# Expert routing rebuilt: logits from the raw residual, norm applied token by token, residual finished inside the first expert

## The reference, cut to what matters

```
mix = (sigmoid(..) * y_attn + sigmoid(..) * y_conv) @ w_out[1]
h = layer_norm(ALPHA * h + mix, ln1_g[1], ln1_b[1])      # called n11 in the kernel
logits = h @ router                                     # 1024 x 8
vals, idx = top_k(logits, 2); gates = softmax(vals)
out = sum over the 8 experts e of combine[:, e] * (silu(h @ wg[e]) * (h @ wu[e])) @ wd[e]
h = layer_norm(ALPHA * h + out, ln2_g[1], ln2_b[1])
```

## Time and profile before

| what | value |
|---|---|
| time, median of 3 runs | 1699.02 us (1697.24 to 1699.38) |
| the profiled execution: time, span | 1695.83 us, 1694.0 us |
| TensorE busy | 1642.3 us, 97% |
| VectorE, ScalarE, GpSimd busy | 1228.0, 969.5, 646.6 us |
| mean granted TensorE clock | 0.989 |
| moved from HBM | 336.76 MB, 199 GB/s |

### The profile page before, as it was taken

One profiled execution on the slowest core, in us unless ns is written; L12 is line 12 of the kernel. 1 busy time (PEld: TensorE's weight loads), 2 busy tenths in 40 slices (PEclk: granted clock), 3 DMA queues, 4 the chain that ended last, 5 costly groups with the idle time before them and its releaser, 6 DMA issues.

```text
span 1694.0 us, 27812 instructions
## 1 busy us (share of the span) xinstructions
PE 1642.3 (97%) x11036; PEld 1485.3 (88%) x11036; DVE 1228.0 (72%) x1837; ACT 969.5 (57%) x1367; POOL 646.6 (38%) x452
## 2 busy tenths in 40 slices
PE   8999999999989999999999999999999999999996
PEld 6988788898878889988899999988888888888885
DVE  6665666666567666998775545899777888788895
ACT  5546575336556634555454433555447777776774
POOL 2333553123345402052110002140138686887863
PEclk9999999999999999999999999999989999999999
DMA  7622455564235555433335445544329898898992
GB/s 283 239 100 100 150 193 187 186 211 169 101 128 196 176 198 199 165 136 139 125 126 198 174 175 175 166 150 150 125 78 337 329 346 328 331 333 327 346 345 104
DMA packets 50200, 339.78 MB, mean 201 GB/s; under 512 B 5575, under 2 KB 7839, under 8 KB 10351
## 3 DMA queue, kind: packets, MB, share of 16 engines
q1 hardware_dynamic: 47344, 328.79, 53.6%
q0 software_dynamic: 2720, 9.13, 1.8%
HBM read 336.76 MB, written 1.13 MB: 199 GB/s over the span
## 4 chain that ended last, share of the span: by engine, by line
PE 82%; DVE 6%; ACT 6%; issue 3%; POOL 2%; DMA 1%; SPq 0%; DVEq 0%; ACTq 0%; POOLq 0%
PE bank L512 12%; PE bank L486 8%; PE bank L488 8%; PE bank L487 8%; PE bank L510 7%; PE bank L930 4%; PE bank L931 4%; PE bank L932 4%; ACT wh L1149 3%; PE bank L643 2%; PE bank L645 2%; PE bank L644 2%; PE bank L961 2%; PE bank L963 2%; PE bank L962 2%
## 5 line engine op out<-in xcount | busy, mean ns | idle before, releaser
L1607 DVE TENSOR_TENSOR wl<-stg,wh 128x2048 fp32r<-128x2048 f32 (+1 forms) x310 | 681.3, 2204 | 255.7 <-ACT wh L1149 254.9
L1149 ACT ACTIVATE wh<-stg 128x2048 fp32r<-128x2048 f32 x310 | 592.1, 1911 | 198.8 <-PE bank L932 82.5
L2301 POOL TENSOR_TENSOR wl<-stg,wh 128x512 fp32r<-128x512 f32 x132 | 322.0, 2453 | 114.9 <-ACT wh L1149 95.9
L486 PE MATMUL bank<-xx,wh 128*128 128x272 f32 (+1 forms) x810 | 235.0, 290 | 1.1 <-DVE xx L2002 1.0
L488 PE MATMUL bank<-xx,wl 128*128 128x272 f32 (+1 forms) x810 | 232.4, 287 | 0.0
L487 PE MATMUL bank<-xx,wh 128*128 128x272 f32 (+1 forms) x810 | 232.3, 287 | 0.0
L512 PE MATMUL bank<-xx,wh 128*128 128x512 f32 x448 | 160.1, 396 | 0.0
L486 PEld LDWEIGHTS bank<-xx,wh 128*128 128x128 f32 x810 | 152.4, 188 | 3.1 <-issue 1.9
L487 PEld LDWEIGHTS bank<-xx,wh 128*128 128x128 f32 x810 | 153.6, 190 | 0.0
L488 PEld LDWEIGHTS bank<-xx,wl 128*128 128x128 f32 x810 | 152.4, 188 | 0.0
L512 PE MATMUL bank<-H,wh 128*128 128x512 f32 x434 | 151.3, 390 | 0.0
(11 more groups left out here) (347 smaller groups left out, 3731.4 us busy)
## 6 DMA issues: line engine op xcount, KB each, us to landing
stg<-in_w SPq DMA_DIRECT2D x310, 1024.0 KB, 4.8
BT<-bias_scratch POOLq DMA_DIRECT2D x3, 1024.0 KB, 11.2
BT<-bias_scratch POOLq DMA_DIRECT2D x1, 2048.0 KB, 13.2
BB<-bias_scratch POOLq DMA_DIRECT2D x2, 1024.0 KB, 6.4
res<-in_x SPq DMA_DIRECT2D x1, 1024.0 KB, 5.8
stg<-in_w SPq DMA_DIRECT2D x2, 512.0 KB, 7.3
BB<-bias_scratch POOLq DMA_DIRECT2D x2, 512.0 KB, 7.4
out<-res SPq DMA_DIRECT2D x4, 256.0 KB, 3.0
```

Of the source, the lines that this page charges most:

```text
L486: pe.matmul(out, wh, xh(kt), start=kt == 0, stop=False)
L1149: act.activation(WH[u % NW][:, :], stg[u % NS][:, :], ACT.Copy).then_inc(*m.inc("w_high", u))
L1607: vec.tensor_tensor(WL[u % NW][:, 0:n], stg[u % NS][:, 0:n], WH[u % NW][:, 0:n].bitcast(F32), ALU.subtract).then_inc(*m.inc("w_low_v", u))
L2301: pool.tensor_tensor(WL[u % NW][:, VW:], stg[u % NS][:, VW:], WH[u % NW][:, VW:].bitcast(F32), ALU.subtract).then_inc(*m.inc("w_low_g", u))
```

## The change

**Constants of the router, made early.** At the head of `dense` VectorE makes `RW`, the router's 64 columns times the gain of each feature, a column of ones beside them, and the router times the bias, and `AB`, the bias times `ALPHA` (four small instructions). After the norm n2 TensorE sums `RW` over all features with ones (8 products of 17 columns, in place of 4 of the 11 warming products) and VectorE copies the 17 sums to `GB`.

**Logits from the raw residual.** The logits of a token are then (raw product - mean * gain sums) * root + bias sums. The raw products (9 columns, the ninth the sum of the token) need no norm, and stand among the sums of mean and variance. No 11 warming products follow.

**Turned tokens normed token by token.** The eight centre, scale and bias steps for all tokens are gone. The root is brought from `BC` to a column for each token by two one-column products; TensorE turns the raw tiles; ScalarE reads a turned bank with scale `RT` and bias `NB` into `ZT` (4 instructions of 128 x 512), and `XTH`, `XTL` are split from `ZT`.

**Gain and bias behind the gathering.** High and low parts are summed in one bank; each of the 8 feature tiles of a pair is read from the bank with its gain and bias into `TK` (even tiles on ScalarE, odd ones on VectorE), copied to `GH` by ScalarE, and subtracted into `GL` by VectorE. The four gathers of pair 0 now stand before the branch.

**Residual inside the first expert.** At `between(0,0)` to `between(1,1)` of expert 0, for two tiles each: VectorE subtracts the mean and scales by gain and root, ScalarE scales by `ALPHA` and adds `AB`.

**Holds.** VectorE holds no splits over `evac_o` in either layer; GpSimd holds from tile 3 (before: tile 5) of the last layer until `top_gap`. ScalarE issues the split at the end of tile 5, ahead of the squares. The table load for Ln and Exp stands one tile earlier. The semaphores of several DMAs are merged.

```diff
@@ tensor_program, route
+                def products(kt):
+                    w.wait_ge(*m.of("res", ("o1", kt)))
                     for tt in range(2):
...
+                        ins = pe.matmul(PS[router][:, tt * 16:tt * 16 + 9], RES[:, kt, M + tt * P:M + (tt + 1) * P], RW[:, kt, 0:9],
+                                        start=kt == 0 and tt == 0, stop=kt == KD - 1 and tt == 1)
...
+                w.wait_ge(*m.of("rstd", name))
+                for tt in range(2):
+                    ins = pe.matmul(PS[b][:, tt:tt + 1], BC[:, M + tt * P:M + (tt + 1) * P], ident[:, 0:1], start=True, stop=True)
...
+                for q in range(4):
+                    gather(0, q, "group")
@@ tensor_program, last_sums
-                keep_warm(11)
+                if name != "n2":
+                    keep_warm(11)
+                    return
...
+                for kt in range(KD):
+                    ins = pe.matmul(PS[b][:, 0:17], ones, RW[:, kt, :], start=kt == 0, stop=kt == KD - 1)
+                ins.then_inc(*m.inc("group", "gains"))
+                keep_warm(7)
@@ scalar_program
+                def sums(nt):
+                    if nt == 5:
+                        sp.enter(sp.at // UT)
+                    shifted(f"n1{l}", nt)
...
+            def take_out(j, kt, sem):
...
+                act.activation(TK[kt % 4], bank(("gather", j, q))[:, kt % 4 * P:kt % 4 * P + 2 * P], ACT.Identity, bias=small("ln1b", KD + kt),
+                               scale=small("ln1g", KD + kt)).then_inc(*m.inc("taken_a", (j, kt)))
+            def gathered_high(j, kt):
...
+                w.wait_ge(*m.of("taken_v" if kt % 2 else "taken_a", (j, kt)))
+                act.activation(GH[j % 2][:, kt, :], TK[kt % 4], ACT.Copy).then_inc(*m.inc("gathered_high", (j, kt)))
+            def residual(kts, scale, bias):
+                for kt in kts:
+                    w.wait_ge(*m.of("resid_y", kt))
+                    act.activation(RES[:, kt, M:T], YT[kt % 4], ACT.Identity, bias=bias(kt), scale=scale).then_inc(*m.inc("resid", kt))
...
+                        act.activation(ZT[:, tt, sl], bank(("xt", tt, q))[:, :], ACT.Identity, bias=NB[:, tt, :],
+                                       scale=RT[:, tt, :]).then_inc(*m.inc("xt_out", (tt, q)))
...
+                        if x == 0 and gi < 2:
+                            residual(range(4 * gi + 2 * late, 4 * gi + 2 * late + 2), ALPHA, lambda kt: AB[:, kt:kt + 1])
@@ vector_program
-                if name[:2] == "n1" and nt == KD - 3:
-                    sp.hold()
-                if name == "n10" and nt == KD - 1:
-                    sp.go_on()
+            def gather(j, q):
+                kts = (4 * (q // 2) + q % 2, 4 * (q // 2) + q % 2 + 2)
+                if q % 2:
+                    for kt in kts:
+                        take_out(j, kt, "group_sp")
...
+                for kt in kts:
+                    gathered_low(j, kt)
+            def residual(kts):
+                for kt in kts:
+                    y = YT[kt % 4]
+                    if kt >= 4:
+                        w.wait_ge(*m.of("resid", kt - 4))
+                    vec.tensor_tensor(y, RES[:, kt, M:T], MEAN[:, M:T], ALU.subtract).then_inc(*m.inc("resid_y", ("centred", kt)))
+                    w.wait_ge(*m.of("resid_y", ("centred", kt)))
+                    vec.scalar_tensor_tensor(y, y, small("ln1g", KD + kt), BC[:, M:T], ALU.mult, ALU.mult).then_inc(*m.inc("resid_y", kt))
@@ gpsimd_program
-                if nt == (KD - 3 if name[:2] == "n1" else KD - 2):
+                if nt == {"n10": KD - 3, "n11": 3}.get(name, KD - 2):
                     sp.hold()
-                if nt == KD - 1:
+                if nt == KD - 1 and name != "n11":
                     sp.go_on()
...
             mix_layer(1)
+            w.wait_ge(*m.of("top_gap"))
+            sp.go_on()
```

More of the change, by code:

```diff
@@ new lines, in gather @@
+            def gather(j, q, sem):
+                k0 = 4 * (q // 2) + q % 2
+                b, old = bank(("gather", j, q), ("taken_v" if q % 2 else "taken_a", (j, k0 + 2)))
+                vacant(old)
+                w.wait_ge(*m.of("xt_low", (1, q // 2)))
+                w.wait_ge(*m.of("chosen", 2 * j + 1))
+                for c in range(2):
+                    kt, n = k0 + 2 * c, 0
+                    for src in (XTH, XTL):
+                        for tt in range(2):
+                            ins = pe.matmul(PS[b][:, c * 2 * P:(c + 1) * 2 * P], src[:, tt, kt * P:(kt + 1) * P], SE[j % 2][:, tt, :],
+                                            start=n == 0, stop=n == 3)
+                            n += 1
+                ins.then_inc(*m.inc(sem, ("gather", j, q)))
@@ L1009, in scatter @@
                         ins.then_inc(*m.inc("group_sp", ("scatter", x, j)))
-                for q in range(4):
-                    gather(0, q)
                 for x in range(8):
@@ L1551, in every_token @@
                 w.wait_ge(*m.of("chosen", 1))
+                residual(range(KD), 1.0, lambda kt: small("ln1b", KD + kt))
                 for kt in range(KD):
+                    w.wait_ge(*m.of("resid", kt))
                     act.activation(XH[:, kt, :], RES[:, kt, :], ACT.Copy).then_inc(*m.inc("again_high", kt))
@@ L2049, in dense @@
             def dense():
+                rw = small("router", 0, 64).rearrange("p (a b) -> p a b", a=KD)
+                for col, name in ((0, "ln1g"), (9, "ln1b")):
+                    vec.tensor_tensor(RW[:, :, col:col + 8], rw, small(name, KD, KD).unsqueeze(2).to_broadcast([P, KD, 8]), ALU.mult)
+                vec.tensor_scalar(AB, small("ln1b", KD, KD), ALPHA, None, ALU.mult)
+                vec.memset(RW[:, :, 8:9], 1.0).then_inc(*m.inc("router_scaled", 0))
                 def evac(i):
@@ L2089, in route @@
             def route():
+                name = "n11"
+                d, v, t = SQ[:, 1, :], SQ[:, 2, :], SQ[:, 3, :]
+                mean, var = bank((name, "mean"))[:, 0:T], bank((name, "var"))[:, 0:T]
                 io, four = iota[:, 0:8], [P, 2, 8, 8]
@@ new lines, in route @@
+                w.wait_ge(*m.last("v_step"))
+                vec.scalar_tensor_tensor(t, t, -0.5, v, ALU.mult, ALU.mult).then_inc(*m.step("v_step"))
+                w.wait_ge(*m.last("v_step"))
+                vec.scalar_tensor_tensor(BC[:, :], t, 1.5, BC[:, :], ALU.add, ALU.mult).then_inc(*m.inc("rstd", name))
+                w.wait_ge(*m.of("group", "router"))
+                sums = bank("router")[:, 0:32].rearrange("p (a b) -> p a b", a=2)
+                vec.tensor_scalar(NM, sums[:, :, 8:9], -1.0 / D, None, ALU.mult).then_inc(*m.step("v_step"))
@@ new lines, in route @@
+                w.wait_ge(*m.last("v_step"))
+                for tt in range(2):
+                    ins = vec.scalar_tensor_tensor(lg[:, tt, :], GB[:, 0:8], NM[:, tt, :], sums[:, tt, 0:8], ALU.mult, ALU.add)
+                ins.then_inc(*m.inc("logits", 0))
+                w.wait_ge(*m.of("group", "root"))
+                vec.tensor_copy(RT, bank("root")[:, 0:2].unsqueeze(2)).then_inc(*m.inc("root_out", 0))
+                w.wait_ge(*m.last("root_out"))
+                vec.tensor_tensor(NB, NM, RT, ALU.mult).then_inc(*m.inc("token_bias", 0))
@@ L2098, in route @@
+                w.wait_ge(*m.last("logits"))
                 for tt in range(2):
-                    w.wait_ge(*m.of("group", ("router", tt)))
-                    vec.tensor_copy(lg[:, tt, :], bank(("router", tt))[:, 0:8]).then_inc(*m.inc("logits", tt))
-                w.wait_ge(*m.last("logits"))
+                    ins = vec.scalar_tensor_tensor(lg[:, tt, :], lg[:, tt, :], RT[:, tt, :], GB[:, 9:17], ALU.mult, ALU.add)
+                ins.then_inc(*m.step("v_step"))
+                w.wait_ge(*m.last("v_step"))
@@ L2132, in route @@
                 choose(1)
+                for tt in range(2):
+                    turned_low(tt, 1)
+                for k0 in (0, 4):
+                    take_out(0, k0 + 1, "group")
+                    take_out(0, k0 + 3, "group")
+                    for kt in range(k0, k0 + 4):
+                        gathered_low(0, kt)
             def gates(tag):
@@ L2209, in between @@
                     def between(gi, late):
+                        if x == 0 and gi < 2:
+                            residual(range(4 * gi + 2 * late, 4 * gi + 2 * late + 2))
                         if x > 0 and gi == 0:
@@ L2232, in every_token @@
                 gates("et")
+                w.wait_ge(*m.of("mean", "n11"))
+                residual(range(KD))
                 for kt in range(KD):
```

232 lines of the change are left out of this document (135 added, 97 removed).

## The result

| kernel | median | runs | ratio to before |
|---|---|---|---|
| before | 1698.2 us | 1697.2 to 1699.4 | |
| after | 1721.7 us | 1719.7 to 1722.4 | 1.0136 [1.0124, 1.0148] |

The change makes the kernel 23.5 us slower. The forecast was 1705 (1690 to 1714): the sign was right, the size was not, and the time lies outside the range. The profiled execution after has a span of 1720.5 us, 26.5 more than the one before.

A forecast was written before the change was run, and what follows sets the result against it. TensorE, busy 97% of the span, was taken as the bound, with little slack for splits in the experts. Terms -1.5 - 5.9 + 12 + 2 = +6.6 gave 1702.4 for the profiled execution, median 1705; own range 1701 to 1711, bounds 1690 to 1714.

The forecast's parts named there:

- Routing: From the last `w_out` product to the first expert product: 5.9 us saved, bounds -10.4 and -4.
- Rival E: Takes, not gathers, set the start of the experts, so routing gives only 2 us: +10.5, 1709.5; chance 0.04.
- The sign and the mechanism of expert 0: Expert 0: slower; ScalarE's splits wait for VectorE's scaling at four stops, 4 to 7 us; five TensorE gaps.
- The first expert: Residual at four stops and (2,0) in expert 0: ScalarE waits for VectorE, next splits late, +12 us (2 to 17).
- rival D: VectorE's centrings at the stops wait for GpSimd, stops cost 16 instead of 12: +10.6, 1709.6; chance 0.14.
- Norm n2: Router constants and 8 narrow sums replacing 4 warming products: nothing, at worst 1 us.
- Later gathers: Experts 2 and 4 lose 1.0 us each at stop (2,0), the others are covered by slack: +2 (0 to 4).
- n10: Norm n10: VectorE's held split moves off the norm's first step, gain 1.5 us (0 to 2).
- A: Rival: stops covered, residual and takes cost TensorE 1 us in all: -6.4, 1692.6; chance 0.22.
- C: Rival: clock stays up, routing -10.4, but stops cost 14: +4.1, 1703; chance 0.08.

The follow-up runs named there:

- experiment 5: Kernel after, VectorE writing 2032 of 2048 low-part columns, GpSimd 16, for units 183 to 190, then 183 to 195: 1722.0 and 1719.9 us.
- experiment 2: Kernel after with ScalarE's residual step one stop behind VectorE's: 1714.0 us; kernel after with the n11 residual left out: 1706.7 us.
- Experiment 1: Kernel after, 7 warming products sharing the gain sums' PSUM bank: 1718.5 us; kernel before, n2's 11 warming products split over two banks: 1705.4 us.
- Experiment 3: Kernel after, but for later pairs ScalarE takes all eight feature tiles out of the banks, VectorE none: 1714.0 us.
- the one with the shared bank: Kernel after, 7 warming products behind norm n2's sums moved ahead of the gain sums into the same PSUM bank: 1718.5 us.

## Why the prediction was right and wrong

**What held.** *Routing*, -5.9 forecast, -7.9 measured, inside the bounds. The comparison follows the root by 1.4 us (1249.69 to 1251.06), and the first gather stands 16.2 us behind the last `w_out` product (before 22.6, 15 to 16 forecast). But the parts are off against each other. The root did not come 2 us nearer: it lies 7.7 us behind the last product, before 7.1, because the mean still waits 1.24 us for GpSimd's sum. In return the clock was low for 3.4 us in all, so the transposes took 2.69 us instead of 3.8, and the gathers, which before had half the clock for 3.1 of their 5.4 us, 3.9 instead of the 5.7 that I gave them. Rival E is out: the first expert product stands 0.24 us behind the last one of the gathers, with no wait, so the gathers set the start and not the takes.

*The sign and the mechanism of expert 0.* ScalarE's splits start 3.7 to 7.8 us after the last one at the five stops, with VectorE's scaling as the releaser (at (2,0) its take), and TensorE has its gaps ahead of 184, 186, 188, 190 and 191. They are 4.0, 1.2, 3.2, 2.2 and 1.1 us, where I had five of 2 to 3.5. `gate_up` took 50.5 us, over the 40 that would have disproved it.

**What failed, in order of size.**

*The first expert: +12, measured +18.8.* The step is "VectorE first ends its own split (1.8 us after ScalarE's)". At (0,1), (1,0) and (1,1) it ends it 2.7 us after, and at (0,0), where three low parts stand in a row behind the first lows and the gates, 4.4. From the end of ScalarE's split to its next one passed 6.6, 6.0, 6.3, 7.8 and 3.7 us, where I had 4.2, 5.0, 4.9, 6.7 and 3.9: 30.3 against 24.7. I had taken the duration of one low part; what stood in its place were two, the second of which takes 2.70 us instead of 1.76, because GpSimd's low part is in its way, and the first centring 0.90 instead of 0.42; with GpSimd's part cut to 16 columns the centring took 0.41 (experiment 5). This is rival D, with more reach than I gave it: I put GpSimd's hindrance at the centrings alone. Of the rule that I named beside it, the Trainium skill's page SBUF — State Buffer, section "Who interferes with whom" (such instructions of VectorE and GpSimd exclude each other for a whole instruction), the trace agrees: GpSimd's 512 columns take 2.83 us beside VectorE, 1.12 of them behind the end of VectorE's 1.76, and its 16 columns took 2.31 beside VectorE's 2.28. The second failure is in how I summed: late by so much, less the slack, as if each stop were a shift against the kernel before. Once the cover is gone ScalarE and VectorE are a loop of their own, and its length, 9.7 us for two units, is the price, not the differences. And a part of it was no wait at all: with ScalarE's step one stop later 8 us of the residual's 15.7 stayed (6.6 if the half-clock stretch in that trace is taken out), VectorE's own load. In the earlier trace rows it has 7 us to spare in 50, and I charged the residual's 4 x 1.9 us to ScalarE's wait alone. The sum itself has a slip: 2.3 + 2.7 + 2.3 + 3.4 + 3.0 is 13.7 and not 13. And 3.1 of the 18.8 us are not the residual's (experiment 2).

*Norm n2: 0, measured +5.8.* The step is "the 8 narrow sums replace 4 warming products: nothing". As work that holds. What I didn't price was the resource that they take, a PSUM bank in a rotation of eight. Experiment 1 shows it in both directions.

*Later gathers: +2, measured +6.3.* The step is "At the others ScalarE is held 1.2 to 1.5 us against 2.1". In the code the gather at (2,0) is number 2k + 1 in every expert, and the odd ones are those that VectorE takes out, so the stop of experts 2 and 4 is that of 1, 3 and 5 too: ScalarE is held 2.6 us there, for takes behind VectorE's split and turned low part. Experiment 3 takes the wait away and the time comes back. It relieves VectorE as well, so that the wait is the likely cause of all of it and not proven to be the only one.

*n10: -1.5, measured +0.35.* The held split did move off the norm, but beside GpSimd's work it takes 2.86 us instead of 2.28, GpSimd's add beside it takes 2.81 us (0.77 to 0.99 for the one at this place and its neighbours before), and TensorE now waits 1.55 us for this running sum. That is read from the trace; no run undid it. Timelines of VectorE, GpSimd and TensorE after:

```profile
853.53 2.86 DVE L1685 TENSOR_TENSOR wl<-stg,wh 128x2048 fp32r<-128x2048 f32 x1
```
```profile
854.20 2.81 POOL L2541 TENSOR_TENSOR xc<-xc,res 128x272 f32<-128x272 f32 x1
```
```profile
857.15 0.70 PE L748 MATMUL bank<-xc,consts 128*128 128x272 f32 x2 [1.55 <-POOL xc L2541]
```

**The rivals.** A is out: the stops weren't covered. C's clock was nearly right (3.4 us at half) and its price wrong. D is the one that the traces of `gate_up` speak for, and its 16 for the stops would have given 1709.6. With the bank and the gathers as measured (+5.8, +4.3) it comes to 1719.7, but that is near the 1721.7 in part by luck: the routing gained 2 us more than forecast, n10 gained nothing, and the stops cost 18.8.

## What to carry to other kernels

A count of instructions doesn't show what an edit takes from a rotation: where buffers go round, name for every added one which later user now gets whose buffer, and when that is freed. Where two engines are made to wait for each other at a stop, add up the whole loop, with each step at the duration that it has beside the third engine's work, and compare it with what the bound engine needs for the same stretch; a slack of the kernel before is no measure. And idle time of the bound engine that happens to match a forecast proves nothing: fill it, and see whether the time goes. Where two traces of the same code differ, follow both place by place before calling it noise: here 1.5 us were a half-clock stretch that fell on another unit.

## What the runs showed of the hardware

*VectorE and GpSimd on SBUF.* A low part of GpSimd's over 16 columns took 2.31 us while VectorE had one over 2032 (2.28). In expert 0 of the kernels in which ScalarE no longer waited, giving GpSimd's quarter to VectorE made the whole 4.4 us faster, twice (1.9 us in expert 0 where no half clock disturbs the pair); in the kernel after it made no difference that can be told.

*Half clock with and without a price.* Three stretches at 1.2 GHz, 3.4 us each, followed TensorE's stalls of 2.2 to 4 us in expert 0; with enough warming products in the stalls they were gone and the kernel was no faster, as in `gate_up` the splits came no sooner. On unit 191 in `down` such a stretch cost 1.2 to 1.6 us: without it 13.1 us passed from this unit to expert 1, and with it 14.3 to 14.7 (five traces).

*A spread ahead of any change.* Between profiles of kernels that are alike in their first 850 us TensorE's products differ by up to 5.6 us at that point. Most of it comes in steps of 1 to 1.8 us: at the start (the first input landed at 6.8 to 8.5 us), near 170 to 188 us, and from 475 to 495 us. Windows at the second place, of the kernel after and of the one with the shared bank, whose code is the same there: 0.92 and 0.84 of the clock, and behind it the second is 1.7 us later than ahead of it.

```profile
168.00:190.00 22.00, 18.45 (x130) 15.53 (x129) 16.52 (x21) 8.83 (x15) 12.40 (x15) 0.92 0.27 98
```
```profile
168.00:190.00 22.00, 18.48 (x120) 15.38 (x119) 16.46 (x21) 8.63 (x14) 12.43 (x15) 0.84 0.28 98
```

Effects of a few us are read from one place of two traces, not from their spans.
